# Up products of a fp32 feed-forward block: high and low parts of the rows side by side, 512 columns wide

## What is computed

```
h   = rmsnorm_2(x, norm_ffn_2)                    # 256 x 1024
up  = h @ w_up_2                                  # 1024 x 5632: two halves of 2816
up  = causal_dwconv(up, ffn_conv_w_2)             # three taps along the 256 tokens, per channel
act = silu(up[:, :2816]) * up[:, 2816:]
x   = x + act @ w_down_2                          # 2816 x 1024
out = rmsnorm(x, norm_final_2)
```

## Time and profile before

| | us |
|---|---|
| median of three runs | 1618.52 |
| profiled execution | 1620.15 |
| its span in the trace | 1618.4 |
| TensorE busy (matmuls) | 1571.4 (97%) |
| VectorE busy | 618.2 (38%) |
| ScalarE busy | 468.2 (29%) |
| GpSimd busy | 286.3 (18%) |

### The profile page before, as it was taken

How to read it: one execution, slowest core, us unless ns; L and a number is a source line. 1 busy time by engine, 2 the same in 40 slices (tenths; PEclk the granted TensorE clock), 3 DMA queues, 4 the chain that set the end, 5 groups by cost and what they waited for, 6 DMA issues and landing times. The chain is left out here.

```text
span 1618.4 us, 22257 instructions
## 1 busy us (share of the span) xinstructions
PE 1571.4 (97%) x9004; PEld 911.6 (56%) x9004; DVE 618.2 (38%) x1149; ACT 468.2 (29%) x703; POOL 286.3 (18%) x179
## 2 busy tenths in 40 slices
PE   9999999999999999999999999999999999999998
PEld 8843333333333333333233233598898899999986
DVE  7742222121212112121121221485586444478852
ACT  6431111111111111101111111466555554454443
POOL 3500000000000000000000000274234324445552
PEclk9999999999999999999999999999999999999999
DMA  9699999999999999999999999634224125555542
GB/s 349 223 381 369 427 426 427 427 428 427 427 427 427 427 427 428 427 428 428 428 428 428 428 427 428 220 141 156 105 105 157 61 97 209 179 172 184 185 179 104
DMA packets 94892, 507.73 MB, mean 314 GB/s; under 512 B 10060, under 2 KB 35449, under 8 KB 70105
## 3 DMA queue, kind: packets, MB, share of 16 engines
q1 hardware_dynamic: 94568, 505.97, 77.4%
q10 hardware_dynamic: 240, 0.55, 0.1%
HBM read 505.46 MB, written 1.05 MB: 313 GB/s over the span
## 5 line engine op out<-in xcount | busy, mean ns | idle before, releaser
L190 POOL TENSOR_TENSOR low<-ring,high 128x1024 fp32r<-128x1024 f32 x81 | 200.5, 2476 | 1272.2 <-ACT high L187 1272.1
L1735 PE MATMUL ps<-ring,x 128*64 128x512 f32 x1536 | 341.9, 595 | 19.9 <-DMA ring<-in_w_up 19.9
L1735 PEld LDWEIGHTS ps<-ring,x 128*64 128x64 f32 x1536 | 106.0, 137 | 251.7 <-issue 207.2
L187 ACT CAST high<-ring 128x1024 fp32r<-128x1024 f32 x162 | 167.8, 1049 | 191.6 <-PE ps L1906 116.9
L1902 PE MATMUL ps<-hTh,high 128*128 128x256 f32 x768 | 189.1, 284 | 0.5 <-PEq L2849 0.5
L1903 PE MATMUL ps<-hTl,high 128*128 128x256 f32 x768 | 188.4, 283 | 0.0
L1777 PE MATMUL ps<-ring,x 128*64 128x512 f32 x752 | 172.0, 600 | 0.8 <-DVE x L1595 0.8
L190 DVE TENSOR_TENSOR low<-ring,high 128x1024 fp32r<-128x1024 f32 x81 | 108.9, 1344 | 129.6 <-ACT high L187 129.5
L1902 PEld LDWEIGHTS ps<-hTh,high 128*128 128x128 f32 x768 | 147.3, 192 | 1.8 <-issue 1.4
L1903 PEld LDWEIGHTS ps<-hTl,high 128*128 128x128 f32 x768 | 147.4, 192 | 0.0
L1580 DVE TENSOR_SCALAR hT<-ps 128x512 f32<-128x512 f32 x32 | 22.1, 691 | 295.3 <-PE ps L1735 295.3
(11 more groups left out here) (503 smaller groups left out, 2091.3 us busy)
## 6 DMA issues: line engine op xcount, KB each, us to landing
ring<-in_w_down SPq DMA_DIRECT2D x52, 2048.0 KB, 32.8
ring<-in_w_gate SPq DMA_DIRECT2D x48, 2048.0 KB, 31.4
ring<-in_w_up SPq DMA_DIRECT2D x47, 2048.0 KB, 31.1
ring<-in_w_in SPq DMA_DIRECT2D x22, 2048.0 KB, 8.1
extra<-in_w_gate SPq DMA_DIRECT2D x16, 2048.0 KB, 31.6
extra<-in_w_up SPq DMA_DIRECT2D x16, 2048.0 KB, 29.8
extra<-in_w_down SPq DMA_DIRECT2D x14, 2048.0 KB, 34.6
ring<-in_w_up SPq DMA_DIRECT2D x24, 1024.0 KB, 6.1
```

Of the source, the lines that this page charges most:

```text
L187: eng.copy(hi, self.raw(u)).then_inc(self.sem("high_split"), 1)
L190: eng.tensor_tensor(lo, self.raw(u), hi.bitcast(F32), ALU.subtract).then_inc(self.sem(who + "_split"), 1)
L1735: last = pe.matmul(bank[h * CAP:(h + 1) * CAP, :], xg[:, c, kh, :], w[:, c, h * 512:(h + 1) * 512], start=False, stop=kh == 1 and c == 3)
```

## The change

In the up products the rows' high and low parts now lie side by side for each of the eight chunks of the contraction: `hTb[:, c, 0, :]` is the high part, `hTb[:, c, 1, :]` the low one, and `hTh` and `hTl` are views of it. With the weights' high part TensorE runs one matmul over all 512 columns instead of two over 256. The sums with the rows' high part stand in the first 256 columns of a bank, the others in the last 256, and the weights' low part adds to those. Each unit fills a bank of its own, four banks a step. In step 0 the first two units keep matmuls of 256 columns (`first_columns_wide`).

The two sums of a unit are put together behind it: ScalarE copies the last 256 columns to the new tile `whole` in SBUF, VectorE adds the first 256 columns to it there and releases the bank, and the taps read `whole`. ScalarE's casts follow one by one behind the copies. A copy waits until the taps of the step before have read its quarter of `whole`.

The buffers `yf` and `yg` have the same side-by-side layout, `wg2_high` and `wg2_low` are moved in them, the bank of the taps is planned after those of the norm, and the semaphores of the small loads are joined: `gb_in` with `wg_in`, and `taps_in` with `rb_in`. (`both_parts` is defined and not called.)

```diff
-        hTh = sb("hTh", [P, KC, S], F32R)
-        hTl = sb("hTl", [P, KC, S], F32R)
+        hTb = sb("hTb", [P, KC, 2, S], F32R)
+        hTh, hTl = (hTb[:, :, i, :] for i in range(2))
...
-        piece("up", (None, ("up", j, 0), None, ("up", j, 1)))
+        piece("up", [("up", j, q) for q in range(4)])
...
+def columns_wide(pe, units, banks, u, keys, xb, before=None, first=None):
+    if first:
+        first_columns_wide(pe, units, banks, u, keys[:2], xb, *first)
+    for q in range(2 if first else 0, 4):
+        bank = banks.claim(pe, keys[q])
+        wh = units.buf(units.high, u + q)
+        wl = units.buf(units.low, u + q)
+        units.high_ready(pe, u + q)
+        for c in range(KC):
...
+            pe.matmul(bank, wh[:, c * P:(c + 1) * P], xb[:, c, :, :].rearrange("p a s -> p (a s)"), start=c == 0, stop=False)
+        units.ready(pe, u + q)
+        for c in range(KC):
+            last = pe.matmul(bank[:, S:2 * S], wl[:, c * P:(c + 1) * P], xb[:, c, 0, :], start=False, stop=c == KC - 1)
+        units.finish(last, u + q)
...
-                pe.wait_ge(sem("wg_in"), 16)
+                pe.wait_ge(sem("gate_weights_in"), 48)
...
-                v.wait_ge(sem("rb_in"), 48)
+                v.wait_ge(sem("small_rows_in"), 16 * 9)
...
-    banks.plan("taps", *[("nn", j) for j in range(4)], ("up", 0, 0), ("up", 0, 1))
+    banks.plan(*[("nn", j) for j in range(4)], "taps", *[("up", 0, q) for q in range(4)])
...
+            def low_sums(j, h):
+                for a in range(2):
+                    bank = banks.take(act, ("up", j, 2 * h + a))
+                    if j:
+                        act.wait_ge(sem("up_conv"), 4 * j - 4 + 2 * h + a + 1)
+                    act.copy(whole[:, h, a, :], bank[:, S:2 * S]).then_inc(sem("up_low"), 1)
+                    units.ahead(act, "high", U0 + 4 * j + 2 * h + a + 1)
             for j in range(NUP):
-                units.ahead(act, "high", U0 + 4 * j + 2)
+                low_sums(j, 0)
                 if j:
                     act.wait_ge(sem("up_act"), j)
                     act.copy(act_high[:, 2 * j - 2:2 * j, :], cv[:, (j - 1) % 2, 1]).then_inc(sem("act_high"), 1)
-                units.ahead(act, "high", U0 + 4 * j + 4)
-                banks.moved(act, ("up", j, 0))
+                low_sums(j, 1)
+                act.wait_ge(sem("up_conv"), 4 * j + 2)
                 act.activation(cv[:, j % 2, 0], cv[:, j % 2, 0], ACT.Silu).then_inc(sem("up_silu"), 1)
...
                 for h in range(2):
-                    units.ahead(v, "low0", U0 + 4 * j + 2 * h + 2)
-                    bank = banks.take(v, ("up", j, h))
+                    for a in range(2):
+                        units.ahead(v, "low0", U0 + 4 * j + 2 * h + a + 1)
+                        bank = banks.take(v, ("up", j, 2 * h + a))
+                        v.wait_ge(sem("up_low"), 4 * j + 2 * h + a + 1)
+                        last = v.tensor_tensor(whole[:, h, a, :], whole[:, h, a, :], bank[:, 0:S], ALU.add)
+                        banks.release(last, ("up", j, 2 * h + a))
                     for i in range(3):
                         for a in range(2):
                             c = cv[:, j % 2, h, a, :]
                             w = taps[:, h, FF_CHUNKS * (2 - i) + 2 * j + a:FF_CHUNKS * (2 - i) + 2 * j + a + 1]
                             if i == 0:
-                                last = v.tensor_scalar(c, bank[:, a * S:(a + 1) * S], w, None, ALU.mult)
+                                banks.moved(v, ("up", j, 2 * h + a))
+                                last = v.tensor_scalar(c, whole[:, h, a, :], w, None, ALU.mult)
                             else:
-                                last = v.scalar_tensor_tensor(c[:, i:], bank[:, a * S:(a + 1) * S - i], w, c[:, i:],
+                                last = v.scalar_tensor_tensor(c[:, i:], whole[:, h, a, 0:S - i], w, c[:, i:],
                                                               ALU.mult, ALU.add)
```

More of the change, by code:

```diff
@@ L410, in build @@
         with ExitStack() as ce:
-            yf = [sb("yf_" + w, [P, KC, S], F32R, ce) for w in ("high", "low")]
-            yg = [sb("yg_" + w, [P, KC, S], F32R, ce) for w in ("high", "low")]
+            yfb, ygb = (sb(w, [P, KC, 2, S], F32R, ce) for w in ("yfb", "ygb"))
+            yf, yg = ([b[:, :, i, :] for i in range(2)] for b in (yfb, ygb))
             X = sb("X", [P, NT, HG, P], stack=ce)
@@ L789, in _ @@
             sp.dma_start(wg[:, :, 0:8], w_in[:, 4 * W:4 * W + 8].rearrange("(c p) n -> p c n", p=P))\
-                .then_inc(sem("wg_in"), 16)
-            sp.dma_start(gb[:, 0:1], A["ig_b"].rearrange("a h -> h a")).then_inc(sem("gb_in"), 16)
-            sp.dma_start(gb[:, 1:2], A["fg_b"].rearrange("a h -> h a")).then_inc(sem("gb_in"), 16)
+                .then_inc(sem("gate_weights_in"), 16)
+            sp.dma_start(gb[:, 0:1], A["ig_b"].rearrange("a h -> h a")).then_inc(sem("gate_weights_in"), 16)
+            sp.dma_start(gb[:, 1:2], A["fg_b"].rearrange("a h -> h a")).then_inc(sem("gate_weights_in"), 16)
             for j, c0 in list(enumerate(IN_COLS))[1:]:
@@ L1017, in _ @@
             conv(0)
-            v.wait_ge(sem("gb_in"), 32)
+            v.wait_ge(sem("gate_weights_in"), 48)
             bank = banks.take(v, "gates")
@@ L1907, in columns, with first_columns_wide, both_parts @@
         units.finish(last, u + q)
+def first_columns_wide(pe, units, banks, u, keys, xb, high_ready, low_ready):
+    bank = [banks.claim(pe, key) for key in keys]
+    high, low = ([b[:, i * S:(i + 1) * S] for b in bank] for i in range(2))
+    wh = [units.buf(units.high, u + i) for i in range(2)]
+    wl = [units.buf(units.low, u + i) for i in range(2)]
+    w = [slice(c * P, (c + 1) * P) for c in range(KC)]
+    for i in range(2):
+        units.high_ready(pe, u + i)
+    units.ready(pe, u)
+    for c in range(KC):
+        high_ready(c)
+        for i in range(2):
+            pe.matmul(high[i], wh[i][:, w[c]], xb[:, c, 0, :], start=c == 0, stop=False)
+        pe.matmul(low[0], wl[0][:, w[c]], xb[:, c, 0, :], start=False, stop=False)
+    for c in range(KC):
+        low_ready(c)
+        last = pe.matmul(low[0], wh[0][:, w[c]], xb[:, c, 1, :], start=False, stop=c == KC - 1)
+    units.finish(last, u)
+    for c in range(KC):
+        pe.matmul(low[1], wh[1][:, w[c]], xb[:, c, 1, :], start=False, stop=False)
+    units.ready(pe, u + 1)
+    for c in range(KC):
+        last = pe.matmul(low[1], wl[1][:, w[c]], xb[:, c, 0, :], start=False, stop=c == KC - 1)
+    units.finish(last, u + 1)
+def columns_wide(pe, units, banks, u, keys, xb, before=None, first=None):
[6 more added lines that the diff above has]
+        units.high_ready(pe, u + q)
+        for c in range(KC):
+            if before and q == 0:
+                before(c)
+            pe.matmul(bank, wh[:, c * P:(c + 1) * P], xb[:, c, :, :].rearrange("p a s -> p (a s)"), start=c == 0, stop=False)
+        units.ready(pe, u + q)
+        for c in range(KC):
+            last = pe.matmul(bank[:, S:2 * S], wl[:, c * P:(c + 1) * P], xb[:, c, 0, :], start=False, stop=c == KC - 1)
+        units.finish(last, u + q)
+def both_parts(v, banks, key, out):
+    bank = banks.take(v, key)
+    last = v.tensor_reduce(out, bank.rearrange("p (a s) -> p s a", a=2), AX.X, ALU.add)
+    banks.release(last, key)
 def rows(pe, units, banks, u, keys, xh, xl, before=None):
@@ L1976, in phase_c @@
 def phase_c(nc, A, sem, sb, ring, banks, k, env):
-    x, xn, hT, ident, tri, ones, prm2, units, hTh, hTl, yf, yg, prm1, prow1, prow2, stat = (
-        env[n] for n in "x xn hT ident tri ones prm2 units hTh hTl yf yg prm1 prow1 prow2 stat".split())
+    x, xn, hT, ident, tri, ones, prm2, units, hTh, hTl, yf, yg, prm1, prow1, prow2, stat, hTb, yfb = (
+        env[n] for n in "x xn hT ident tri ones prm2 units hTh hTl yf yg prm1 prow1 prow2 stat hTb yfb".split())
     eps2 = sb("eps2", [P, 1])
@@ L2035, in phase_c @@
     wg2 = X.rearrange("p t h n -> p (t h) n")
-    wg2_high, wg2_low = (yf[0][:, 4 * i:4 * i + 4, :].rearrange("p c (a n) -> p (c a) n", a=2) for i in range(2))
+    wg2_high, wg2_low = (yfb[:, 2 * i:2 * i + 2].rearrange("p c b (a n) -> p (c b a) n", a=2) for i in range(2))
     kbg = sb("kbg", [P, HG, P])
@@ L2082, in _ @@
             for i, name in enumerate(("fox_f_bias_2", "gdn_a_log_2", "gdn_dt_bias_2")):
-                sp.dma_start(rb[:, i:i + 1], A[name].rearrange("a h -> h a")).then_inc(sem("rb_in"), 16)
+                sp.dma_start(rb[:, i:i + 1], A[name].rearrange("a h -> h a")).then_inc(sem("small_rows_in"), 16)
             for h, prow in enumerate((prow1, prow2)):
@@ L2087, in _ @@
                                  A["ffn_conv_w_2"][0, i, h * FF_CHUNKS * P:(h + 1) * FF_CHUNKS * P]
-                                 .rearrange("(c p) -> c p", p=P)).then_inc(sem("taps_in"), 16)
+                                 .rearrange("(c p) -> c p", p=P)).then_inc(sem("small_rows_in"), 16)
             sp.wait_ge(sem("wg2_zeroed"), 1)
```

(29 more changed lines are left out.)

## The result

The changed kernel takes 1640.93 us (median of four runs, 1639.21 to 1641.59) against 1618.52 before: a ratio of 1.0134, 95% interval 1.0122 to 1.0146, 22.4 us slower. The forecast was 1640.7. The profiled execution of after is the lowest of its runs, 1639.21 us with a span of 1637.5.

The account below looks back on a forecast made before the run. TensorE bounds the kernel before; after, VectorE's 9.2 us plus 4.5 blocked by GpSimd make steps of 13.6 us, shifting the end by 22.2: 1618.52 + 22.2 = 1640.7 us, range 1620 to 1652 (0.82).

Parts of the forecast that it names:

- VectorE's own step: Up products: VectorE's work in one step, 8.52 us plus about 0.65 for eight waits, 9.2 us without blocking.
- Prices: Up products, VectorE from SBUF: multiply-add 0.48 us, multiply 0.35, add 0.41; ScalarE's copy 0.372.
- Blocked time: Up products: VectorE stands still for GpSimd 0.34 + 2.14 + 1.98 = 4.5 us a step, making 13.6 us.
- the walk: A settled step of the up products followed instruction by instruction, SBUF going to whoever asked first: 13.6 us.
- The signs to look for: Up products: multiply-adds of 0.48 us with two a half near 2.5; product to product 13.6 us, not 11.1.
- the sum: Up products: ten steps of 13.6 us, the first 2.3 longer, the last 2.1 shorter; total shift +22.2 us.
- The chain through VectorE: VectorE reaches the first step at 1436.64; the low of the fifth down chunk ends at 1585.3 with the gaps.
- the small edits: Joined load semaphores, bank order, layout of hTh and yf: no effect; at worst 5 us if the first DMA took 16.
- The 4.5 us that the wide matmuls save: Up products, TensorE: 0.0134 us less for each of 8 pairs in 42 units, lost again because TensorE waits.
- Its waits: Up products: TensorE waits at the second halves of the even units, 1.0 and 1.55 us a step.

Follow-up runs that it names:

- GpSimd's fills: The changed kernel with three GpSimd scratch fills of 870 columns in place of each of its lows of the up products: 1617.22 us, 0.9988.
- the kernel with sums in PSUM: The changed kernel, but VectorE's add writes its sum back to the PSUM bank and the taps read it there: 1614.96 us, 0.9975.

## Why the prediction was right

The forecast took VectorE's own step and the time that GpSimd blocks it, and made TensorE follow. Each term can be read from the trace of after, and the experiments show the mechanism. That the median falls within 0.3 us of the forecast is in part luck: the runs of after alone spread over 2.4 us.

- **Prices.** Multiply-adds 0.48 (483 ns at the median), multiplies 0.35 (343), adds 0.41 (412), ScalarE's copies 0.37: all from rows of before where the instruction stood elsewhere. The scalar from a tile mattered: priced by the product's 0.69, which has none, a multiply-add would have been set at 0.42, 0.06 shorter, eight times a step.
- **Blocked time.** 4.5 us a step forecast. In the step shown it is (4.03 - 1.78) + (3.88 - 1.78) + (0.99 - 0.61) = 4.7, in a step of 13.5 it is 4.5 (3.82, 3.88 and 0.98 in the same places). The places are those of the walk: one pair of multiplies by `act_low`, one multiply-add of each half by a low. The signs to look for said two blocked multiply-adds a half, against the walk, and the walk had it right. The settled step is 13.57 in the mean for 13.6, the first 2.3 longer and the last 2.1 shorter, as the sum had them.
- **The chain through VectorE.** From `taps` to the low of the fifth down chunk 148.7 us forecast; 1433.59 to 1581.83 is 148.2. Before it was 126.5 up to that chunk on TensorE. The difference, 21.8, is the loss in this pair of executions; `taps` of the one of after began 3.05 us earlier, which is why its total is 19.1 above and not 22. The first matmul behind units 0 and 1 starts between 1427.5 and 1430.9 in the seven kernels with the wide layout, and at 1430.4 before. With such a spread among kernels that share the small edits, these traces can't tell whether the edits gain a microsecond or nothing.
- **TensorE.** The 4.5 us that the wide matmuls save were 3.8, and they are lost in the changed kernel, as forecast. Its waits were set at 2.55 us a step; 13.52 less four units of 2.79 leaves 2.36.
- **Not said.** GpSimd blocks VectorE in the kernel before as well: the product loses 0.66 us a step and one of the two lows 0.69 (1.91 at 1492.85, for 1.22). After, they take 0.69 and 1.22: GpSimd's instructions no longer fall on them. The walk had it so without a word.
- **Who blocks whom.** Beside GpSimd's fills a VectorE low keeps its 1.22 us and a multiply-add its 0.48; beside GpSimd's subtractions a multiply-add takes up to 2.71. A multiply from SBUF to SBUF waits for both kinds, 0.72 us beside `act_low` and 0.74 or 1.07 beside fills in the settled steps, instead of 0.34. The rule of the Trainium skill (SBUF — State Buffer, "Who interferes with whom") says the same, two SBUF inputs against GpSimd's reading and a two-port mode against any access. The runs bear out both halves, but no row shows the mode in which the multiplies run.
- **Copying first.** From one multiply to the next it is 0.27 us from SBUF and 0.40 from PSUM, and yet the taps from SBUF cost 15.7 us by themselves in this kernel, because GpSimd works beside them. The other rule of the Trainium skill (VectorE: DVE Perf Modes, "Rules for kernel authors"), to copy from PSUM to SBUF first for many operations, fits the first number; the time here decides against it.

## What to carry to other kernels

Before moving an operand of VectorE's from PSUM to SBUF, add up the time in which GpSimd reads SBUF in the same stretch. That time and the time of VectorE's instructions with two SBUF inputs, and of its multiplies from SBUF to SBUF, add; they don't overlap. GpSimd's writing counts against the multiplies alone. Here 6.1 us of GpSimd and 7.2 us of VectorE met in a step for which TensorE needs 11.2. A shorter instruction that loses its PSUM input can be a longer step; writing the sum back to PSUM kept the gain.

## What the runs showed of the hardware

- GpSimd is held up as well: `act_low` takes 1.56 us where it starts during a VectorE low, instead of 1.28, and once 2.28 in the second step.
- 512-column matmuls of split operands follow each other by 0.230 us in groups of eight between groups of 256-column ones, by 0.2266 in a row of their own, and those of plain fp32 by 0.43 (L1332 in the kernel before, from 83.1 us on).
- A fill of 870 columns by GpSimd leaves a VectorE low of 1024 columns at 1.22 us, while a subtraction by GpSimd lengthens it: 1.99 in the kernel with sums in PSUM, beside `act_low`.
